# Permuted expert slots, and ScalarE's final squares behind its last weight cast, in a one-core recurrent, retention and mixture-of-experts trunk

## What is computed

```python
g_top, grp = top group of 4;  topi = the 2 best experts of the 8 in that group
for each expert e, xb = the rows of its tokens:
    h = silu(xb @ w_gate[e]) * (xb @ w_up[e])        # 1024 x 512, twice
    y = h @ w_down[e]                                # 512 x 1024
    out[row_tok] += y * row_w[:, None]
h = h + ffn
y = rms_norm(h, norm_final_g)
```

## Time and profile before

| what | us |
|---|---|
| median of 3 runs | 1877.16 |
| lowest, highest | 1875.75, 1878.24 |
| the profiled execution, whole | 1877.87 |
| its span, first to last instruction | 1875.9 |
| TensorE busy in the span | 1790.4 (95%) |
| mean share of the clock granted to TensorE | 0.979 |
| DMA: bytes moved | 316.47 MB |

### The profile page before, as it was taken

One profiled execution on the slowest core, in us unless ns is written; L12 is line 12 of the kernel. 1 busy time (PEld: TensorE's weight loads), 2 busy tenths in 40 slices (PEclk: granted clock), 3 DMA queues, 4 the chain that ended last, 5 costly groups with the idle time before them and its releaser, 6 DMA issues. The chain is left out here.

```text
span 1875.9 us, 25694 instructions
## 1 busy us (share of the span) xinstructions
PE 1790.4 (95%) x10105; PEld 1552.0 (83%) x10105; DVE 1066.5 (57%) x1242; ACT 774.3 (41%) x911; POOL 519.0 (28%) x293
## 2 busy tenths in 40 slices
PE   9999999999999999999999979989999999999962
PEld 7989989999999999999999968757777777777641
DVE  8565580002455544555611142468888888998856
ACT  5455550001212211122300032247878878777743
POOL 0422322223222222222222210022323433323224
PEclk9999999999999999999999989989999999999986
DMA  4111112223111111111222456469999999999973
GB/s 147 38 51 51 45 40 69 68 69 119 44 37 39 42 36 36 36 38 32 60 92 92 159 190 241 163 269 330 376 374 371 379 365 376 379 368 370 372 272 113
DMA packets 146514, 316.47 MB, mean 169 GB/s; under 512 B 11153, under 2 KB 106481, under 8 KB 121720
## 3 DMA queue, kind: packets, MB, share of 16 engines
q1 hardware_dynamic: 135896, 287.74, 42.1%
q0 software_dynamic: 10528, 27.48, 5.3%
HBM read 288.12 MB, written 36.47 MB: 173 GB/s over the span
## 5 line engine op out<-in xcount | busy, mean ns | idle before, releaser
L222 PE MATMUL job_ps<-xn_hi,w_hi 128*128 128x352 f32 x1488 | 494.7, 332 | 0.3 <-issue 0.3
L224 PE MATMUL job_ps<-xn_hi,w_lo 128*128 128x352 f32 x1488 | 478.6, 322 | 0.0
L223 PE MATMUL job_ps<-xn_lo,w_hi 128*128 128x352 f32 x1488 | 477.9, 321 | 0.0
L206 POOL CAST w_hi<-w_raw 128x1024 fp32r<-128x1024 f32 x78 | 85.6, 1098 | 774.2 <-issue 467.2
L222 PEld LDWEIGHTS job_ps<-xn_hi,w_hi 128*128 128x128 f32 x1488 | 279.9, 188 | 4.1 <-issue 1.0
L223 PEld LDWEIGHTS job_ps<-xn_lo,w_hi 128*128 128x128 f32 x1488 | 280.5, 189 | 2.5 <-issue 0.2
L224 PEld LDWEIGHTS job_ps<-xn_hi,w_lo 128*128 128x128 f32 x1488 | 279.8, 188 | 0.0
L2377 DVE TENSOR_TENSOR ex_raw_lo<-ex_raw,ex_w_hi 128x2048 fp32r<-128x2048 f32 x88 | 202.1, 2310 | 13.3 <-ACT ex_w_hi L2244 12.0
L208 POOL TENSOR_TENSOR w_lo<-w_raw,w_hi 128x1024 fp32r<-128x1024 f32 x78 | 205.0, 2629 | 6.3
L754 DVE TENSOR_TENSOR gate<-job_ps,gate 128x352 f32<-128x352 f32 x48 | 25.2, 525 | 288.5 <-PE job_ps L224 288.5
L2244 ACT ACTIVATE ex_w_hi<-ex_raw 128x2048 fp32r<-128x2048 f32 x86 | 165.0, 1918 | 53.5 <-PE ex_y L2113 20.3
(11 more groups left out here) (331 smaller groups left out, 3391.9 us busy)
## 6 DMA issues: line engine op xcount, KB each, us to landing
ex_raw<-in_w_chunks SPq DMA_DIRECT2D x88, 1024.0 KB, 22.6
u<-in_w_chunks SPq DMA_DIRECT2D x52, 1024.0 KB, 19.5
raw_more<-in_w_chunks SPq DMA_DIRECT2D x52, 1024.0 KB, 20.5
w_raw<-in_w_in SPq DMA_DIRECT2D x64, 512.0 KB, 4.0
merged_lru<-gate SPq DMA_DIRECT2D x8, 528.0 KB, 5.0
spare<-merged_lru SPq DMA_DIRECT2D x8, 528.0 KB, 5.9
merged<-gate SPq DMA_DIRECT2D x8, 528.0 KB, 5.0
w_raw<-in_w_lru_o SPq DMA_DIRECT2D x8, 512.0 KB, 4.1
```

Of the source, the lines that this page charges most:

```text
L206: pool.tensor_copy(M.w_hi[s][:], M.w_raw[s][:]).then_inc(M.hi_done[s], 1)
L222: pe.matmul(out, M.w_hi[s][:, k, :], x_hi[:, k, cols], start=(k == 0), stop=False)
L223: pe.matmul(out, M.w_hi[s][:, k, :], x_lo[:, k, cols], start=False, stop=False)
L224: mm = pe.matmul(out, M.w_lo[s][:, k, :], x_hi[:, k, cols], start=False, stop=(k == KD - 1))
```

## The change

A new constant table of 96 columns, `CN_SLOT`, holds for each slot the rank that it takes: slot s takes rank (s mod 6) * 16 + s / 6 (whole division), so that rank r stands in slot (r mod 16) * 6 + r / 16. `place` compares the rank with this table in place of 0 to 95. The shape and count of all instructions stay; the small constants are 617 columns wide and not 521. With 66 tokens, slots 0 to 65 were filled before; now of each run of six slots (6j to 6j+5) the first four or five are.

Apart from it, `last_step` has another order, and VectorE's first `turned_round` stands two instructions later.

```diff
+CN_SLOT = CN_TOK + NTILE
+CN_N = CN_SLOT + SLOTS
+DMA_ENGINES = 16
...
+    slot, share = np.arange(SLOTS), SLOTS // DMA_ENGINES
+    cn[:, CN_SLOT:CN_SLOT + SLOTS] = (slot % share * DMA_ENGINES + slot // share)[None, :]
...
-                dve.tensor_tensor(in_slot[k][:, ts], R.const[:, CN_IOTA:CN_IOTA + SLOTS].unsqueeze(1)
+                dve.tensor_tensor(in_slot[k][:, ts], R.const[:, CN_SLOT:CN_SLOT + SLOTS].unsqueeze(1)
...
         def last_step():
             act.wait_ge(ss_set, 1)
             act.wait_ge(used, N_CHUNKS - RAW + 6)
-            square_tile(0)
             hi(LAST - 1, 4)
             silu(LAST)
             h_part(LAST - 1)
+            hi(LAST, 4)
+            act.activation(warm[:], R.eps[0:1, :], ACT.Sqrt)
+            square_tile(0)
+            h_part(LAST)
             square_tile(1)
             square_tile(2)
-            act.activation(warm[:], R.eps[0:1, :], ACT.Sqrt)
-            hi(LAST, 4)
             root(0)
-            h_part(LAST)
             for i in range(3, 6):
                 square_tile(i)
...
         lo(LAST, 4)
-        turned_round(0)
         h_part(LAST)
         lo(LAST, 5)
+        turned_round(0)
```

More of the change, by code:

```diff
@@ L90 @@
 CN_TOK = CN_IOTA + P
-CN_N = CN_TOK + NTILE
+CN_SLOT = CN_TOK + NTILE
+CN_N = CN_SLOT + SLOTS
+DMA_ENGINES = 16
 NOWHERE = float(1 << 20)
```

## The result

The changed kernel takes 1859.41 us (median of 4 runs, 1856.28 to 1859.66), against 1876.45 for the kernel before (median of 4, 1872.46 to 1878.24): ratio 0.9908, 95% interval 0.9889 to 0.9928. It is faster by 17.0 us. The profiled execution took 1859.66, with a span of 1857.8, and lies 18.2 us under the profiled one of before. Forecast were 24.6 us and 1853.0; the direction and most of the mechanism hold, the time lies in the stated range of 1848 to 1862, and 6.4 us are missing.

A forecast was written before the change was run, and what follows sets the result against it. Transfers falling behind TensorE through uneven rows on DMA engines were taken as the cause; 5.1 (steps) + 17.2 (stall) + 2.3 (gain wait) = 24.6 us off 1877.87 gave about 1853.0 us, range 1848 to 1862.

The forecast's parts named there:

- The bound: Expert steps and end: uneven rows make DMA transfers fall behind, costing 5.1 us in steps and some 17 at the end.
- shares of six neighbours: Indirect row transfers: 96 slots go to 16 engines six in a row, so the first carry 6 + 6 rows an expert.
- Steps: 5.1 us: Expert steps: with even rows TensorE never runs dry of weights, gaining 5.1 us; landings some 20 us at the end.
- price of a row: DMA engine time for one gathered or added row: 0.33 us taken, 0.265 us kept as the other end.
- the prediction's sum: Fullest DMA engine's time per expert: 15.0 us of weights plus its rows, 12 before and 9 after, times the row price.
- The 18.98: Steps before the change: the slowest DMA engine was said to need 18.98 us for one expert, against TensorE's 17.67.
- The stall at the end: 17.2 us: Last step: VectorE starts on chunk 191 at 1814.9, not 1837.22; 17.2 us of the 22.3 come from the stall.
- the written-out end: Last step's engine-by-engine schedule from estimated durations, adding 1.0 us for GpSimd beside VectorE; last low part starts at 1814.9.
- VectorE's wait for a gain: 2.3 us: End: GpSimd starts its gains 24.9 us earlier against VectorE's 22.3, so VectorE's 2.33 us wait goes, gaining 2.3 us.
- What is moved costs nothing: Last step: moved squares, reciprocal and table load hold nobody up; second root at 1819.1, asked for at 1820.8.
- the first rival: Steps and end: the backlog stays and only the new order works, gaining 12 us, to 1865; chance 0.13.
- Slower, rows dearer on all engines at once: Steps: spread rows hold each other up; at 0.53 us a row 12 us are lost, 1889 us; chance 0.04.

The follow-up runs named there:

- e1: Kernel before plus the constant table alone, squares and turned round in the old order: 1856.69 us, ratio 0.9894 to the kernel before.
- e10: e8 with rank r left in slot r (no permuted table), old order kept: 1873.35 us, ratio 0.9983 to the kernel before.
- e3: Changed kernel with rank r in slot (r mod 8) * 12 + r / 8, full shares on every second engine: 1866.07 us, ratio 0.9943.
- e4: Changed kernel with rank r in slot 95 - r, full shares on the last engines: 1867.57 us, ratio 0.9944 to the kernel before.
- e8: e7 with squares and first reciprocal back in the old order: 1849.24 us, ratio 0.9847 to the kernel before.
- e5: Changed kernel with the cast of chunk 187 moved from GpSimd to ScalarE, ahead of that of 188: 1856.32 us, ratio 0.9889.
- e6: e5 with the cast of chunk 191 also moved from GpSimd to ScalarE: 1855.68 us, ratio 0.9878 to the kernel before.
- e7: e6 with no gains on GpSimd, VectorE multiplying all nine tiles: 1854.05 us, ratio 0.9873 to the kernel before.

## Why the prediction was right, and where it wasn't

- *The bound: an uneven load of rows on DMA engines, one backlog behind both losses.* Right. e1 has the whole gain, e10 loses it, and e3 and e4 keep six filled slots in some shares and change only which, and bring 33.5 and 30.5 us of landing. The prediction took the shares of six neighbours as given, and no row of the kernel before showed them. Of the maps compared they alone fit these landings and the landing marks of e3, where eight of a chunk's 16 come within 11.3 us and eight at 29.0 to 33.5. Which share is the first and which the last isn't shown.
- *Steps: 5.1 us.* 5.0 measured (535.41 to 530.41). In the 29 steps of the table three executions with natural slots took 517.37, 519.50 and 520.22 us, and the seven with even ones 512.44 to 512.71, so the gain is 4.7 to 7.8 us, by which executions are compared, and that 5.0 comes so near to 5.1 is in part luck. Landings were to be about 20 us at the end and are 15.1 at 1750 to 1790. Neither price of a row was measured: the backlog grew unevenly, see above. Before, from the turn at 1624.88 to that of step 31 at 1806.68, landings stood at 33 to 34 us until 1750 and TensorE waited for weights, so transfers set the pace, at 18.18 us a step and not 18.98; by the prediction's sum that is 0.265 us a row. The 18.98 was the mean of a slower and a faster growth.
- *The stall at the end: 17.2 us.* 14.5 measured: from the turn of step 31 to the start of the last low part it was 30.54 us before (1806.68 to 1837.22) and is 16.08 (1803.01 to 1819.09); the sum had 13.3. This is the term that was mis-sized, by 2.8 us. The step that failed is the written-out end, which took GpSimd as there in time for each cast, and added only 1.0 us for its work beside VectorE. In e8 the last low part begins 11.5 us after the SiLU of expert 31, as the sum had it (1803.5 to 1814.9), and in the changed kernel 14.0. Of the 2.5 between them, e5 shows 0.7 for the late cast of 187, and e6 another 1.4 for the cast of 191, which VectorE waited for; the rest was not taken apart.
- *VectorE's wait for a gain: 2.3 us.* Wrong: 2.34 us are still there. The prediction had chunk 191 cast by 1812.3 and the gains from there; the cast waited for TensorE until 1814.44 and took 4.61 us. TensorE began the down part of expert 30 at 1811.31 and not at 1807.5; 1.4 us of that is the late first turn, and 2.0 are the two waits of 1.04 and 0.98 us in its rows, which the sum didn't have; 0.4 are not accounted for. e6 shows that an earlier start wouldn't have done it: GpSimd's first gain was held up there until VectorE's low parts were done.
- *The rest, 1.3 us,* is the late first turn. It is none of the change's: the kernels that share the code spread by 6.3 us there. 5.0 + 14.5 - 1.3 = 18.2. What lies behind the start of the last low part is the same in both, 38.7 us to the end of the span.
- *What is moved costs nothing.* Right for the changed kernel: VectorE takes the second root at 1824.87, 3.1 us after it was there (1821.73; the forecast had 1.7). e7 and e8 show that the squares behind the last cast cost 2.2 us once VectorE is quicker.
- *The new order as part of the gain.* The prediction gave the order a value of its own only in the first rival, 12 us to 1865. With the backlog it is 7.5 by medians (1869.64), 9.3 in the stretch at the end. That rival was wrong as to the changed kernel.
- *Slower, rows dearer on all engines at once.* Excluded: TensorE is busy in 80.00 of 80 us at 1700 to 1780, where it should have starved.

What stays open: why the landings grow so unevenly (in the changed kernel not at all until 1500 us, and hardly after 1600), what a row costs an engine, which share lies on which engine, and why the first part of the program differs by up to 6.3 us between executions.

## What to carry to other kernels

When transfers fall behind with a DMA share of 1.00, ask how the rows of an indirect transfer fall on the 16 engines before giving up on bandwidth: here 96 slots went in shares of six (e3), and rank r in slot (r mod 16) * 6 + r / 16 was worth 5 us in the steps and more at the end. A fix of a cause can leave a fix of its symptom without use, so test each alone: moving the squares was worth 7.5 us with the backlog, nothing without it, and cost 2.2 when the end was made shorter. And an engine that helps another is to be priced with both side by side.

## What the runs showed of the hardware

In these rows GpSimd and VectorE beside each other don't slow down in part: one stands until the other's instruction is done. The last low part of the changed kernel starts at 1819.09, 0.06 us behind the first of GpSimd's gains, which takes 2.35 us (the three start at 1819.03 and the second part of them, in the chain of waits, at 1821.35); 1821.35 + 2.27 = 1823.62, and it ends at 1823.57. In e5 the low parts of 188 and 189 start 0.14 us behind GpSimd's cast (1803.11, 1.90 us): 1.76 + 4.48 = 6.24, measured 6.10. The other way round, the cast of 191 in the changed kernel starts at 1814.44 while VectorE is in the addition, goes on with the low part of 190 to 1817.30, and takes 4.61 us; alone it takes 1.90, and 1819.05 - 1.90 = 1817.15. The scaling of a tile took 2.76 us with a gain beside it, and 0.74 without, in one execution. The prediction's 1.0 us for it was about half of one such wait (2.26 us, from 1819.09 to 1821.35).

One row goes further. The first gain of e6 starts at 1812.45, beside VectorE's addition, and takes 7.77 us. It doesn't get in behind the addition (1813.07), nor behind the low part of 190 (1815.28), but only behind that of 191 (1817.94): 1817.94 + 2.35 = 1820.29, and it ends at 1820.22. So it stood through three VectorE instructions that started after it (the low part of 190, the hidden low part, the low part of 191) and followed each other without a gap. Why it didn't get in between isn't shown.

The gathers of GpSimd are held up too. In the rows above they start at 1797.29 and 1800.40, inside the low parts that run to 1799.26 and 1802.18, and end 0.84 and 0.84 us behind those; the first one starts 0.36 us ahead of a low part and ends 0.86 us behind it. The first gather of e6 starts 0.39 us ahead of a low part (1792.15 to 1792.54) and gets through in 0.98 us; its other two end 0.84 and 0.84 us behind low parts. So a gather that got through in 0.98 us once takes GpSimd up to 3.50 when VectorE forms low parts, and a cast that stands behind three of them is late.
